# Groups C and D of a streaming encoder step: queries prepared by ScalarE and GpSimd, every mask of D added by VectorE

## The reference

```
C: scores = q k^T / 8 + T5 bias, over the block's own key tile and the one before; softmax with a sink
D: score = sum_h w_h relu(qi_h . ki);  sel = the 256 best keys of each query
   scores = q k^T / 8 + T5 bias, over the selected keys;  softmax;  times v   (one k and v for all 8 heads)
```

## Time and profile before

| | |
|---|---|
| median of 3 runs | 4170.81 us (4169.08 to 4173.33) |
| the profiled execution, its span | 4172.25 us, 4170.4 us |
| PE, DVE, ACT, POOL busy over the span | 91%, 50%, 39%, 17% |
| attention C, attention D | about 3025 to 3226 us, 3226 to 3917 us of the span |

### The profile page before, as it was taken

One profiled execution on the slowest core, in us unless ns is written; L12 is line 12 of the kernel. 1 busy time (PEld: TensorE's weight loads), 2 busy tenths in 40 slices (PEclk: granted clock), 3 DMA queues, 4 the chain that ended last, 5 costly groups with the idle time before them and its releaser, 6 DMA issues. The chain is left out here.

```text
span 4170.4 us, 51477 instructions
## 1 busy us (share of the span) xinstructions
PE 3779.2 (91%) x18129; PEld 2628.8 (63%) x18129; DVE 2094.3 (50%) x4989; ACT 1609.7 (39%) x2441; POOL 689.1 (17%) x408
## 2 busy tenths in 40 slices
PE   4899999996999999997999788999868599999798
PEld 3689988995776666665874544444345355555476
DVE  3211111117887344343320199999868766665432
ACT  5111000113454444433320189996445243333332
POOL 4100000002222111111430000000032542211143
PEclk9999999997999999998999899999979699999899
DMA  5222212215455333213431211111242311100243
GB/s 182 66 74 79 67 65 77 68 57 116 98 117 112 72 68 75 65 32 109 163 123 66 63 29 61 61 42 55 97 110 77 89 47 25 37 11 3 107 161 126
DMA packets 222512, 328.50 MB, mean 79 GB/s; under 512 B 22225, under 2 KB 129033, under 8 KB 220897
## 3 DMA queue, kind: packets, MB, share of 16 engines
q1 hardware_dynamic: 173280, 236.21, 19.8%
q10 hardware_dynamic: 43776, 72.50, 4.7%
q0 software_dynamic: 5216, 16.70, 1.9%
HBM read 214.35 MB, written 110.99 MB: 78 GB/s over the span
## 5 line engine op out<-in xcount | busy, mean ns | idle before, releaser
L1028 PE MATMUL attAB_p_o<-attAB_pt,attAB_v 128*65 128x512 f32 (+3 forms) x1120 | 432.8, 484 | 0.2 <-ACT attAB_pt L1075 0.2
L1115 DVE TENSOR_REDUCE attAB_mx<-attAB_p_s 128x1 f32<-128x512 f32 (+2 forms) x360 | 209.5, 609 | 305.7 <-PE attAB_p_s L963 195.0
L508 DVE COPY ab_stage<-ab_pA 128x256 f32<-128x256 f32 (+1 forms) x108 | 56.5, 523 | 602.9 <-PE ab_pA L477 572.3
L2394 DVE TENSOR_SCALAR_CACHE_REDUCE cd_junk<-score,cd_thr 128x512 bf16<-128x512 f32 (+8 forms) x288 | 350.4, 1275 | 1.3 <-DVE cd_thr L2411 0.2
L2432 ACT ACTIVATE cd_gate<-score,cd_thr 128x384 bf16<-128x384 f32 (+2 forms) x192 | 322.3, 1679 | 23.8 <-DVE cd_thr L2411 16.6
L506 ACT ACTIVATE ab_stage<-ab_pA 128x256 f32<-128x256 f32 (+1 forms) x108 | 50.0, 463 | 699.8 <-PE ab_pA L477 679.5
L475 PE MATMUL ab_pA<-ab_W_hi,h_hi 128*128 128x256 f32 x1088 | 309.1, 284 | 3.2 <-PE ab_pA L477 3.1
L1005 PE MATMUL attAB_p_t<-attAB_q_a,attAB_k_a 128*128 128x512 f32 (+3 forms) x560 | 300.2, 540 | 12.7 <-DVE attAB_s_t L1160 11.3
L476 PE MATMUL ab_pA<-ab_W_lo,h_hi 128*128 128x256 f32 x1088 | 307.9, 283 | 0.0
L477 PE MATMUL ab_pA<-ab_W_hi,h_lo 128*128 128x256 f32 x1088 | 307.9, 283 | 0.0
L1637 PE MATMUL attD_p_o<-attD_pt,attD_v 128*65 128x512 f32 x548 | 282.6, 597 | 0.0
(11 more groups left out here) (352 smaller groups left out, 8556.0 us busy)
## 6 DMA issues: line engine op xcount, KB each, us to landing
attAB_raw<-t_k SPq DMA_DIRECT2D x32, 640.0 KB, 7.3
attAB_raw<-t_q SPq DMA_DIRECT2D x32, 640.0 KB, 9.6
t_qg<-cd_stage SPq DMA_DIRECT2D x74, 256.0 KB, 2.0
ab_W_raw<-in_w_ab SPq DMA_DIRECT2D x17, 1024.0 KB, 5.8
mix_o<-t_o SPq DMA_DIRECT2D x34, 512.0 KB, 4.3
t_q<-ab_stage ACTq DMA_DIRECT2D x40, 256.0 KB, 2.0
t_k<-ab_stage ACTq DMA_DIRECT2D x40, 256.0 KB, 2.0
norm_x<-in_x ACTq DMA_DIRECT2D x17, 512.0 KB, 3.7
```

The costliest lines, as they stand in the source:

```text
L1028: done = nc.tensor.matmul(p_o[u % 2][0:VW, i0 * P:(i0 + n) * P], left, pt[c % NPT][:, at * P:(at + n) * P], start=(c == plan.chunks_of[u][ ...
L2394: nc.vector.tensor_scalar(junk[nth % 2][:, 0:widths[n]], sc[n][:], T[:, n:n + 1], None, ALU.is_ge, ALU.add, accum_out=cnt[s % 2][:, n:n + ...
```

## The change

The factor 1/8 moves into `project_cd`, where ACT brings the query units out of the banks. In both attention stages ACT then rounds the queries without a factor, and in a second instruction copies rows 0 to 65 from `q_raw` into `q_b` (L1701 of the new kernel). POOL no longer copies; it subtracts to get the low part (L1488 of the new kernel), with waits on its own earlier instructions ahead of it and one on the subtraction behind it. DVE's `split_queries` is gone. PE's first fill of a block and SP's query loads wait for the copy too. `by_dve` is set for all chunks, so PE's identity matmul is never issued, and DVE adds 128 more masks.

```diff
--- before.py
+++ after.py
@@ BlockPlan.__init__
-        self.by_dve = [t >= self.chunks[self.chunks_of[u][-1]][1] - 1 or t % 2 == 1 for u, t in self.chunks]
+        self.by_dve = [True for _ in self.chunks]
...
-        self.split_at = [[] for _ in range(NT)]
...
-                    self.split_at[max(min(ready + 2, first_fill[u] - 1), ready)].append(p)
@@ attention_by_blocks, query_loads (SP)
                 sp.wait_ge(q_split, b - NRAW + 1)
+                sp.wait_ge(q_copied, b - NRAW + 1)
@@ attention_by_blocks, GpSimd
+                own = {}
+
                 def prepare(b):
                     s = b % NQ
                     pool.wait_ge(q_rounded, b + 1)
-                    nc.gpsimd.tensor_scalar(q_b[s][:], q_a[s][0:AUX].bitcast(F32), only_q[:, 0:1], None, ALU.mult
-                                            ).then_inc(q_copied, 1)
+                    if kind == "D" and b:
+                        pool.wait_ge(near_q, b)
+                    for last, n in own.items():
+                        pool.wait_ge(last, n)
+                    nc.gpsimd.tensor_tensor(q_a[s][HD:P], q_raw[b % NRAW][HD:P], q_a[s][HD:P].bitcast(F32), ALU.subtract
+                                            ).then_inc(q_split, 1)
+                    pool.wait_ge(q_split, b + 1)
...
                     done.then_inc(near_k, 1)
+                    own[near_k] = b + 1
...
+                    own[sink_less] = u + 1
@@ attention_by_blocks, fill (PE)
                         pe.wait_ge(q_split, b + 1)
+                        pe.wait_ge(q_copied, b + 1)
@@ attention_by_blocks, round_queries (ScalarE)
-                    nc.scalar.activation(q_a[b % NQ][:], q_raw[b % NRAW][:], ACT.Copy, scale=HD ** -0.5).then_inc(q_rounded, 1)
+                    nc.scalar.activation(q_a[b % NQ][:], q_raw[b % NRAW][:], ACT.Copy).then_inc(q_rounded, 1)
+                    nc.scalar.activation(q_b[b % NQ][:], q_raw[b % NRAW][0:AUX], ACT.Copy, scale=only_q[:, 0:1]).then_inc(q_copied, 1)
@@ attention_by_blocks, VectorE
-                def split_queries(b):
-                    s = b % NQ
-                    dve.wait_ge(q_copied, b + 1)
-                    nc.vector.scalar_tensor_tensor(q_a[s][HD:P], q_raw[b % NRAW][HD:P], HD ** -0.5, q_a[s][HD:P].bitcast(F32),
-                                                   ALU.mult, ALU.subtract).then_inc(q_split, 1)
...
-                for b in plan.early_blocks:
-                    split_queries(b)
...
-                    for b in plan.split_at[c]:
-                        split_queries(b)
@@ project_cd, evacuate (ScalarE)
-                    nc.scalar.activation(stage[u % 2][:, 0:w], pA[u % BANKS][:, 0:w], ACT.Copy).then_inc(ev[u % BANKS], 1)
+                    scale = HD ** -0.5 if u < 2 * TUNITS else 1.0
+                    nc.scalar.activation(stage[u % 2][:, 0:w], pA[u % BANKS][:, 0:w], ACT.Copy, scale=scale
+                                         ).then_inc(ev[u % BANKS], 1)
```

## The result

The changed kernel takes 4123.96 us (median of 4 runs, 4123.08 to 4125.21) against 4171.64 of the kernel before (4169.08 to 4173.33, 4 runs on the same chip): ratio 0.9887, 95% interval 0.9871 to 0.9903. 4121 was forecast, in a range of 4105 to 4148. The profiled execution took 4125.21 (span 4123.4), 47.0 less than the profiled one of before. Where they went is not where the forecast put them all: from its first instruction to its last D takes 636.1 us instead of 686.0, 49.9 less, and C takes 201.9 instead of 198.4, **3.5 more**, where 10.5 less was forecast.

What follows compares the result with a forecast made beforehand. PE was taken to bound mid-D and DVE to bound C, with a third bound in the openings. Terms 29.4 + 5 + 3.5 + 3 + 1.5 + 9 - 1.5 = 49.9 us gave 4121 us as median, range 4105 to 4148.

Steps and rivals of the forecast that it cites:

- Masks, 29.4 us: In D, 128 mask matmuls leave PE, each worth 0.23 us between ends of rows: 29.4 us gained.
- Adds, 0: In D, the 128 added mask adds on DVE hide behind PE's steps and cost 0 us.
- DVE takes PE's place: Rival: in D each added add holds PE for its 0.69 us, 88.6 in all, total 4209 us; chance 0.07.
- ACT's second copy, -1.5 for C and D: ACT's second query copy, 1.1 us each, 17 in D and 17 in C, costs 1.5 us in all.
- ACT in front: Rival: two copies in a row delay the exponential in C and D, 27 us back, total 4148 us; chance 0.11.
- C's 14 blocks, +9: 14 more blocks of C go from 9.08 to 8.4 us, PE being next after DVE: 9 us gained (0 to 17).
- C's opening, +1.5: At the start of C, 2.84 + 1.22 us becomes 2.35: 1.5 us gained (0 to 1.7).
- D's opening, +5, +3.5 and +3: Gains in D from query splits leaving DVE: 5 us at the opening, 3.5 in third and fourth block, 3 in later blocks.
- POOL's split, 0: The query split on POOL, 2.35 us in place of a copy of 2.84, costs 0 us through its new place.
- POOL's split is late: Rival: PE's first fill waits for POOL's subtraction, 34 x 1.1 = 38 us, total 4159 us; chance 0.05.
- good end: Rival that the openings and C give their best gains, total 4103 us; chance 0.07.

Runs made afterwards that it cites:

- masks alone: Kernel before with one line changed, so VectorE adds the mask of every key tile of D, queries prepared as before: 4149.73 us against 4171.00.
- queries alone: Kernel after, but with the masks of D divided between PE and VectorE as before: 4149.99 us (ratio 0.9950).
- Near waits: Kernel before with one wait added: POOL starts `near` of a block of D only when VectorE has split that block's queries: 4158.10 us against 4171.00.
- near behind the keys: Kernel after with C's second copy two steps later; in D POOL starts `near` of the second block only after the cached keys' split: 4110.73 us against 4169.81.

## Why the prediction was right, and where it was not

The time was met within 3 us, but two errors of opposite sign helped, so that it came so close is in part luck.

- **Masks, 29.4 us:** 28.1, or 0.22 us for each of 128. The distance of the ends of rows was the price, not the 391 ns of the row.
- **Adds, 0:** right, with room of at least 0.42 us for each. It needed the splits gone from VectorE: with them the same adds cost 6.8 us (masks alone). "DVE takes PE's place" is refuted for this kernel; even with every add made twice the kernel is 0.15% faster than before.
- **ACT's second copy, -1.5 for C and D:** this step failed. Its reason was that the "copies follow a run of steps with fills, in which ACT is ahead by more than a step". In D that holds: nothing was lost there. In C it doesn't: between two copies lie four steps, with fills in every other one, and the next exponential came 1.8 us late for PE's cover of 0.7 (2.18 us of copies; 1.1 us of PE's wait). The rival "ACT in front", put at 0.8 us for 34 blocks, is true for 13 of C's blocks, at 1.1 us: 14.3 us.
- **C's 14 blocks, +9:** -3.8 (from -0.2 at exponential 0 to +3.6 at 63; -2.5 to -2.8 in the other three profiles with the same C), outside the bounds of 0 to 17. The bound itself was right: 8.4 us a block was forecast for PE, and 9.42 - 1.1 = 8.3; with the copy placed two steps later the block measured 8.54, of which about 0.2 is still wait. The 9.08 from which the 8.4 was subtracted lies 0.14 above the mean of before. I had put the next limit at PE and not asked what ACT's new work does at that very place.
- **C's opening, +1.5:** 0.2. On VectorE the first maximum stands there behind the split of the second keys, which ends at 3058.76 and whose load the change does not touch.
- **D's opening, +5, +3.5 and +3:** 9.0, 6.7 and 5.4, read from queries alone at exponentials 0, 3 and 20: 21.1 where 11.5 were taken. All three lie within their bounds (2 to 11, 1.0 to 6.9, 0 to 13.1). I took middle values between ends far apart. Near waits shows that splits that no longer meet `near` are worth 13 without anything moved.
- **POOL's split, 0:** right in mid-D; "POOL's split is late" is refuted there.

The terms that failed: 9 + 1.5 forecast for C became -3.5 (-2.1 at best), 13 to 14 us too good; D's opening was 9.6 us too poor. The range had its good end from 6 for D's later blocks and 13 for C, where the bounds given were 13.1 and 17; with those it would have been about 4092 and not 4103.

That L1764 (now L1774) would still meet POOL's work was right. Its 4.66 us end 2.14 behind the end of `near`, about the time that it takes alone (2.28 in near behind the keys), and POOL's next, `near_t`, then took 8.38 us for three, where near behind the keys has 6.32. That each waits for the other's whole instruction is what the Trainium skill, "SBUF — State Buffer", section "Who interferes with whom", states; by it the opening would gain less than with the two apart, and in near behind the keys, where the two are apart, the gain left is 0.9 us in the profile, with the later `near` paid for.

## What to carry to other kernels

When work moves to an engine that is far from busy, look at what stands behind it in that engine's order in every stage, not at its busy share: the same two copies were free in D and cost 1.1 us a block in C, and about 0.2 once one stood two steps later. A matmul is worth the distance that it adds between ends, and an engine's long instructions are worth a look at what ran on its neighbour at that time: one wait gained 13 us. When a change is a sum of parts in several stages, run them apart, since a right total can hide a part that loses.

## What the runs showed of the hardware that was not expected

A VectorE split that met POOL's back-to-back instructions did not get the first gap between them in the kernel before (9.24 us, past `near` and two `near_t`), while the split of the cached keys after the change got the first one (4.66 us). What decides which gap it gets stays open. In near waits the split of the cached keys began 0.05 us ahead of `near` and took its own 2.28 us, and `near` took 6.18 where it took 4.07 after the change: there the one that came first went first. The add of 512 columns takes 691 ns and that of 256 columns 424, so halving a VectorE instruction saved 39%, not 50.
